# Two attentions keep unscaled probabilities; a block of ones beside the values gives the row sums in the other 64 partitions, VectorE divides once a head

## The reference, cut to what matters

```python
# latent attention: 8 heads, 96 wide queries and keys, 64 wide values, 512 x 512 scores a head
sc = jnp.einsum('bqhd,bkhd->bhqk', qi, k) * scale
p = jax.nn.softmax(sc, axis=-1).astype(v.dtype)
return jnp.einsum('bhqk,bkhd->bqhd', p, v)

# neighbourhood attention: 8 heads of 64, a window of 8 rows x 16 columns of keys, with a bias
sc = jnp.einsum('bnqhd,banchd->bhnqac', qb, kb) * scale + bias[None]
sc = jnp.where(col_valid[None, None, :, :, None, :], sc, -jnp.inf)
p = jax.nn.softmax(sc, axis=(-2, -1)).astype(v.dtype)
o = jnp.einsum('bhnqac,banchd->bnqhd', p, vb)
```

## Time and profile before

| | us |
|---|---|
| median of 3 runs | 3701.93 |
| lowest, highest run | 3698.83, 3705.82 |
| the profiled execution | 3697.52 |
| its span, first to last instruction | 3695.7 |
| PE busy | 3154.2 (85%) |
| DVE busy | 1556.0 (42%) |
| ACT busy | 1083.0 (29%) |
| POOL busy | 962.2 (26%) |
| DVE, the multiplications of L658 in these four attentions, x128 | 141.2, mean 1103 ns |

### The profile page before, as it was taken

How to read it: one execution, slowest core, us unless ns; L and a number is a source line. 1 busy time by engine, 2 the same in 40 slices (tenths; PEclk the granted TensorE clock), 3 DMA queues, 4 the chain that set the end, 5 groups by cost and what they waited for, 6 DMA issues and landing times.

```text
span 3695.7 us, 32882 instructions
## 1 busy us (share of the span) xinstructions
PE 3154.2 (85%) x12970; PEld 2158.7 (58%) x12970; DVE 1556.0 (42%) x2571; ACT 1083.0 (29%) x1563; POOL 962.2 (26%) x329
## 2 busy tenths in 40 slices
PE   5888997867777755999999879996999999879996
PEld 4666654652222224676665568885767674568885
DVE  8895645441011025444455542213353545642213
ACT  3422304210000012444526222212452625322221
POOL 2362200201000012433212223432443211124441
PEclk9889899878999986999999989998999999989998
DMA  5114320237999981212121112221212121112220
GB/s 228 69 57 160 148 80 23 80 137 315 422 422 422 422 345 39 70 57 80 46 80 45 47 69 93 101 92 59 89 52 80 46 80 46 36 67 103 92 103 34
DMA packets 70077, 465.26 MB, mean 126 GB/s; under 512 B 8656, under 2 KB 8944, under 8 KB 17712
## 3 DMA queue, kind: packets, MB, share of 16 engines
q1 hardware_dynamic: 59184, 436.29, 30.7%
q0 software_dynamic: 5056, 16.55, 1.3%
q10 hardware_dynamic: 5696, 10.49, 0.8%
HBM read 450.70 MB, written 12.60 MB: 125 GB/s over the span
## 4 chain that ended last, share of the span: by engine, by line
PE 64%; DVE 16%; DMA 12%; ACT 3%; issue 2%; POOL 1%; SPq 0%; ACTq 0%; DVEq 0%; POOLq 0%
PE ps L414 13%; PE ps L416 12%; PE ps L415 12%; DMA mring<-w 10%; PE ps L403 4%; PE ps L632 3%; PE ps L615 2%; PE ps L616 2%; PE ps L617 2%; PE ps L746 2%; PE ps L2017 1%; PE ps L643 1%; DMA wring<-wfirst 1%; POOL w_lo L471 1%; DVE rnn L1592 1%
## 5 line engine op out<-in xcount | busy, mean ns | idle before, releaser
L471 POOL TENSOR_TENSOR w_lo<-wring,w_hi 128x2048 fp32r<-128x2048 f32 x176 | 816.3, 4641 | 1906.8 <-ACT w_hi L463 1906.7
L414 PE MATMUL ps<-x_hi,w_hi 128*128 128x512 f32 (+1 forms) x1512 | 615.2, 407 | 50.7 <-POOL w_lo L471 28.8
L416 PE MATMUL ps<-x_hi,w_lo 128*128 128x512 f32 (+1 forms) x1512 | 602.9, 399 | 0.0
L463 ACT ACTIVATE w_hi<-wring 128x2048 fp32r<-128x2048 f32 x176 | 335.6, 1910 | 556.0 <-PE ps L414 392.1
L415 PE MATMUL ps<-xf_lo,w_hi 128*128 128x512 f32 x1112 | 441.8, 397 | 0.0
L414 PEld LDWEIGHTS ps<-x_hi,w_hi 128*128 128x128 f32 (+1 forms) x1512 | 293.0, 194 | 130.0 <-issue 38.1
L416 PEld LDWEIGHTS ps<-x_hi,w_lo 128*128 128x128 f32 (+1 forms) x1512 | 292.7, 194 | 63.6
L2017 PE MATMUL ps<-mring,xT__89 128*64 128x512 f32 x512 | 244.8, 609 | 66.2 <-DMA mring<-w 61.2
L2018 PE MATMUL ps<-mring,xT__89 128*64 128x512 f32 x512 | 245.0, 609 | 0.0
L415 PEld LDWEIGHTS ps<-xf_lo,w_hi 128*128 128x128 f32 x1112 | 214.9, 193 | 43.3
L1835 DVE TENSOR_TENSOR hid<-ps,sil 64x512 f32<-64x512 f32 x32 | 21.8, 682 | 441.6 <-ACT sil L1488 441.6
(11 more groups left out here) (412 smaller groups left out, 5333.8 us busy)
## 6 DMA issues: line engine op xcount, KB each, us to landing
mring<-w SPq DMA_DIRECT2D x192, 1024.0 KB, 28.5
wring<-wlayers SPq DMA_DIRECT2D x148, 1024.0 KB, 4.8
wring<-wfirst SPq DMA_DIRECT2D x60, 1024.0 KB, 4.9
wmodS<-wmod SPq DMA_DIRECT2D x4, 2048.0 KB, 18.5
y_rows<-ysb ACTq DMA_DIRECT2D x64, 128.0 KB, 6.4
rp<-rpb POOLq DMA_DIRECT2D x16, 192.0 KB, 2.6
hT<-xT SPq DMA_DIRECT2D x1, 2048.0 KB, 18.3
xS<-xT SPq DMA_DIRECT2D x1, 2048.0 KB, 7.7
```

What stands on the lines that cost most here:

```text
L414: said(pe.matmul(bank, wh[:, 0:m], hi[:, k, :], start=(k == 0), stop=False))
L416: ins = pe.matmul(bank, wl[:, 0:m], hi[:, k, :], start=False, stop=(k == nk - 1))
L463: act.activation(w_hi[:, q % HI_SLOTS, :], wring[:, g % SLOTS, :], ACT.Copy).then_inc(hi_rdy, 1)
L471: pool.tensor_tensor(w_lo[:, slot % SLOTS, :], wring[:, slot % SLOTS, :], w_hi[:, q % HI_SLOTS, :].bitcast(F32), ALU.subtract).then_inc(lo ...
```

## The change: what it does

In units marked "summed" (neighbourhood and latent attention):

- ScalarE's exponential no longer accumulates a row sum, and VectorE's norm of each unit (L657, L658) is not run. The transposes wait for the exponential alone.
- total writes into pair B, and beside each product with the values it runs a product with a 128x64 block of ones into the other 64 partitions of the same bank. These then hold, 64 times over, the row sum of each query.
- VectorE runs divide(h) once a head: the reciprocal of these 64x512 sums from PSUM into o2, then its product with the 64x512 result in PSUM. It stands behind the maximum of unit 4h+6, and for the last head behind the loop.
- ScalarE doesn't copy the head's result; it only waits for the total before it overwrites PT2.
- heads_split stands ahead of the wait for the last gate tile.

In the neighbourhood attention the product with ones takes up to 512 queries at once: three of them a head (512, 512 and 256 columns), beside the ten of 128 columns with values.

```diff
@@ units_pe
-                    pe.wait_ge(p_norm, k + 1)
+                    if "summed" in u:
+                        pe.wait_ge(exp_done, k + 1)
+                    else:
+                        pe.wait_ge(p_norm, k + 1)
@@ units_dve
+            def divide(h):
+
+                r = 64 * (h % 2)
+                b = B.take(dve)
+                after(dve, dve.reciprocal(o2[r:r + 64, h // 2, :], b[64 - r:P - r, :]), dve_step, "dstep")
+                dve.tensor_tensor(o2[r:r + 64, h // 2, :], b[r:r + 64, :], o2[r:r + 64, h // 2, :], ALU.mult).then_inc(B.free, 1)
+                dve.wait_ge(B.free, B.took)
...
-                if i >= 1:
+                if i >= 1 and "summed" not in u:
                     norm(i - 1)
-            norm(U - 1)
+                if i >= 6 and i % 4 == 2 and "summed" in u:
+                    divide(u["h"] - 1)
+            if "summed" in u:
+                divide(u["h"])
+            else:
+                norm(U - 1)
@@ units_act
+                    if "summed" in u:
+                        act.activation(Pb[:, k % 3, 0:n], src, ACT.Exp, bias=negmax[:, k % 4:k % 4 + 1], scale=sc).then_inc(exp_done, 1)
...
-                    sums(units[i - 3])
+                    if sums is not None:
+                        sums(units[i - 3])
+                    else:
+                        act.wait_ge(B.full, pv_before + units[i - 3]["h"] + 1)
@@ na_units
-                    b = A.claim(pe)
-                    for n, (lo, hi) in enumerate(NA_KEYS):
-                        for j in range(lo, hi):
-                            ins = pe.matmul(b[r:r + 64, n * P:(n + 1) * P], v2[:, j, h * 64:(h + 1) * 64],
-                                            PT2[:, j - lo, n * P:(n + 1) * P], start=(j == lo), stop=(j == hi - 1))
-                    ins.then_inc(A.full, 1)
+                    b = B.claim(pe)
+                    x, width = PT2, max(hi - lo for lo, hi in NA_KEYS)
+                    for j in range(width):
+                        wide = [n for n, (lo, hi) in enumerate(NA_KEYS) if hi - lo > j]
+                        q = slice(wide[0] * P, (wide[-1] + 1) * P)
+                        pe.matmul(b[64 - r:P - r, q], ones[:, 0:64], x[:, j, q], start=(j == 0), stop=(j == width - 1))
+                        for n in wide:
+                            lo, hi = NA_KEYS[n]
+                            ins = pe.matmul(b[r:r + 64, n * P:(n + 1) * P], v2[:, lo + j, h * 64:(h + 1) * 64], x[:, j, n * P:(n + 1) * P],
+                                            start=(j == 0 and n == 0), stop=(j == width - 1 and n == wide[-1]))
+                    ins.then_inc(B.full, 1)
@@ mla_units
-                    b = A.claim(pe)
+                    b = B.claim(pe)
                     for j in range(NQB):
-                        ins = pe.matmul(b[r:r + 64, :], vM[:, j, h * 64:(h + 1) * 64], PT2[:, j, :], start=(j == 0), stop=(j == NQB - 1))
-                    ins.then_inc(A.full, 1)
+                        pe.matmul(b[r:r + 64, :], vM[:, j, h * 64:(h + 1) * 64], PT2[:, j, :], start=(j == 0), stop=(j == NQB - 1))
+                        ins = pe.matmul(b[64 - r:P - r, :], ones[:, 0:64], PT2[:, j, :], start=(j == 0), stop=(j == NQB - 1))
+                    ins.then_inc(B.full, 1)
@@ layer_act
-            def mla_out(u):
-                r = 64 * (u["h"] % 2)
-                act.activation(o2[r:r + 64, u["h"] // 2, :], A.take(act)[r:r + 64, :], ACT.Copy).then_inc(A.free, 1)
-            units_act(act, mla_units(), mla_out, P2, PT2, ml_gates)
+            units_act(act, mla_units(), None, P2, PT2, ml_gates, pv_before=B2 + l * B_LAYER + B_MLA)
@@ layer_dve
             units_dve(dve, mla_units(), P2)
-            a += HEADS + DC - EARLY
+            a += DC - EARLY
+            heads_split()
             dve.wait_ge(A.free, a)
-            heads_split()
```

More of the change, by code:

```diff
@@ L675, in units_dve, with units_act @@
                     dve.tensor_scalar(m, m, u["scale"], None, ALU.mult).then_inc(mx_rdy, 1)
-                if i >= 1:
+                if i >= 1 and "summed" not in u:
                     norm(i - 1)
-            norm(U - 1)
+                if i >= 6 and i % 4 == 2 and "summed" in u:
[4 more added lines that the diff above has]
+                norm(U - 1)
             cnt["dv2"] += U
-        def units_act(act, units, sums, Pb=Pb, PT=PT, between=None):
+        def units_act(act, units, sums, Pb=Pb, PT=PT, between=None, pv_before=None):
             U = len(units)
@@ L692, in units_act @@
                     src, sc = (Lb[:, k % 2, 0:n], 1.0) if "bias" in u else (ps[:, 4 + k % 2, 0:n], u["scale"])
-                    act.activation(Pb[:, k % 3, 0:n], src, ACT.Exp, bias=negmax[:, k % 4:k % 4 + 1], scale=sc,
-                                   accum_out=rsum[:, k % 4:k % 4 + 1]).then_inc(exp_done, 1)
+                    if "summed" in u:
+                        act.activation(Pb[:, k % 3, 0:n], src, ACT.Exp, bias=negmax[:, k % 4:k % 4 + 1], scale=sc).then_inc(exp_done, 1)
+                    else:
+                        act.activation(Pb[:, k % 3, 0:n], src, ACT.Exp, bias=negmax[:, k % 4:k % 4 + 1], scale=sc,
+                                       accum_out=rsum[:, k % 4:k % 4 + 1]).then_inc(exp_done, 1)
                 if between is not None:
@@ L714, in na_units @@
                 for n, (lo, hi) in enumerate(NA_KEYS):
-                    units.append({"nk": hi - lo, "qb": n, "h": h, "scale": NA_SCALE,
+                    units.append({"nk": hi - lo, "qb": n, "h": h, "scale": NA_SCALE, "summed": True,
                                   "q": qk2[r:r + 64, h // 2, n * P:(n + 1) * P], "k": qk2[r:r + 64, 4 + h // 2, lo * P:hi * P],
@@ L1197, in build @@
         A2 = RC + 2 * RC + KVC + 4 + 1 + 1 + RC + 2 * DC + HEADS + HEADS + 2 * NQB + HEADS + 2 * NQB
-        A_LAYER = 4 + 8 + HEADS + DC + 4 + 8 + 4 + DC + MQC + KVC + 1 + HEADS + HEADS // 2 + NQB + HEADS + DC + FFC
+        A_LAYER = 4 + 8 + DC + 4 + 8 + 4 + DC + MQC + KVC + 1 + HEADS + HEADS // 2 + NQB + DC + FFC
+        B2 = 2 + DC + 2 + DC + DC + 2 + 1 + 1 + DC + 2 + 1 + 2
+        B_MLA = HEADS + DC + 8 + 2 * 4 + DC + 2 * 2 + 1 + HEADS
+        B_LAYER = B_MLA + HEADS + DC + DC + 3 + FFC + DC + 3
         cnt["rp"] = 0
```

9 lines of the change are left out of this document (5 added, 4 removed).

## The result

The kernel after takes 3733.26 us (median of 4 runs, 3728.88 to 3733.88), the kernel before took 3701.05 us beside it. The ratio is 1.0086 (95% interval 1.0074 to 1.0098): 27 to 36 us slower. The profiled execution has a span of 3731.8 us, against 3695.7.

What follows compares the result with a forecast made beforehand. PE, busy 85% of the span, was taken as the bound. Neighbourhood +6.25 and latent +11.4 us a layer, +35.3 in two layers, took 3697.5 to 3732.8 us, the median to 3737; range 3700 to 3785.

Steps and rivals of the forecast that it cites:

- stretched multiplications gone: Neighbourhood attention: the norm's multiplications (L658), held until GpSimd's L471 is through, leave PE's path; 5.6 us less a layer.
- wait in 7 heads: Neighbourhood attention: the divide delays the next unit's exponential, so PE waits 0.7 us a head; 4.8 us a layer.
- ones: Products with ones in the totals: 0.3 us a neighbourhood head, 0.1 a latent one; 2.4 and 0.8 us a layer.
- unit 26: Latent attention: the score waiting behind the divide comes 5.96 instead of 3.38 us after T; cost 2.0 us.
- unit 30: Latent attention: the last total comes 7.25 instead of 4.90 us after the scores' start; cost 2.35 us.
- The slope from 4 to 10 elements: Reciprocal's length: 6.0 ns an element, 3.2 us for 512; the 1 to 4 slope gave 4.4; 3.3 taken.
- The rival of the fast reciprocal: Every divide: at one element a step it takes 1.55 us, no head waits; 3698 us, 3691 with free ones; 13%.
- The rival of eight steps an element: Every divide: the reciprocal takes 4.4 us, the high bound at 8.3 ns an element; 14%.
- The clock: Behind each attention a 5.5 us pause halves PE's clock; 1.1 us neighbourhood, 1.3 latent including its last total.
- The rival of the slack: Slack hides the waits in the heads and the clock holds; only stalls, ends and last divides remain; 3712 us; 8%.
- The rival in which the columns of values and ones run in turn: Totals: products with ones and values don't run beside each other; 84 us more, 3821 us; 5%.
- The contention of GpSimd with the divide: Divides held by GpSimd: some three hits a layer of up to 4.5 us on top, inside the range.

Runs made afterwards that it cites:

- no_ones: The kernel after with the products with ones left out in both attentions, the reciprocal reading the rows of values instead, output not divided by the sums: 3734.16 us.
- pieces: The kernel after with each head's divide cut into four pieces of 128 columns behind maxima of following units, the last head's left whole: 3703.53 us.
- warm: The kernel after with idle 128x512 products of constants on PE at the attention ends, 8 in each latent end, 6 of them behind every last total: 3720.48 us.
- copy_recip: The kernel after with a plain copy of the same rows in place of the reciprocal, output not scaled rightly: 3696.25 us.
- twice_recip: The kernel after with the same reciprocal issued twice in a row, result unchanged: 3899.59 us.
- spread: The kernel after with ScalarE's row sums, one 128x4 inversion a head, and four PE products spreading the inverses instead of products with ones: 3700.96 us.

## Why the prediction held, step by step

3737 was predicted, 3733.26 measured. From the first attention on the profiles differ by +33.8 us, the sum was +35.3. The parts fit less well: with what follows it, the neighbourhood attention of layer 0 costs 3.1 us, predicted 6.25, and the latent one 14.1 us, predicted 11.4. The signs came as named: a reciprocal of 3.355 us, no neighbourhood head over 13.4 us, 5.4 us between the last total and the first o_hi matmul. The mechanism was right, and that the total came out this near is in part luck.

| step, us a layer | predicted | measured, layer 0 |
|---|---|---|
| reciprocal 64x512 | 3.3 each | 3.355 each |
| N: stretched multiplications gone | -5.6 | -5.6 |
| N: wait in 7 heads | +4.8 | +4.2 |
| N: last divide | +3.55 | +3.5 |
| N: ones | +2.4 | 0 (no_ones) |
| N: clock behind it | +1.1 | +1.0 |
| L: first units, and 5 gated heads | -0.6 + 2.0 | +2.0 in sum |
| L: unit 26 | +2.0 | +2.0, and 1.5 of clock |
| L: unit 30 | +2.35 | +3.0 |
| L: last divide | +3.55 | +3.5 |
| L: ones | +0.8 | 0 (no_ones) |
| L: clock, last total and behind | +1.3 | +2.1 |

The measured numbers are differences of the rows above to the earlier trace rows. In N the 7 heads are 7 x (13.32 - 12.72), and the stage's +2.1 us is 4.2 + 3.5 - 5.6. In layer 1 the stages are +0.7 and +14.8: before lost some 1.5 us to a fall of the clock inside its N1 and none in the last total of its L1. In L a gated head, one with gate pieces beside it, takes 15.01 to 15.03 instead of 14.50 us.

- **The reciprocal.** The slope from 4 to 10 elements was the right one of the two. From 128 to 512 elements it is (3351 - 956) / 384 = 6.24 ns an element (pieces). The rival of the fast reciprocal said 3698 or 3691; with a copy in its place it is 3696. The rival of eight steps an element, at 4.4 us, is excluded.
- **The waits.** The arithmetic of slack, divide plus bias, maximum and exponential against the time until PE wants the score, held for the steady heads within 0.15 us. The unit 26 wait was put at 5.96 us from the start of the scores behind the total to the score that waits; it is 2055.17 - 2049.28 = 5.89.
- **Unit 30** was put 0.65 us too low, and for a reason that could have been read from the code: ScalarE's order puts the copy of unit 29's transposed block behind the exponential of unit 31, and the last transposes need the bank that it frees. Before, the norm ran on DVE beside that copy (0.50 us); without the norm PE waits for the copy itself, at 2069.01.
- **The ones** were taken for 3.2 us a layer too much. Their price was a guess between bounds, and the lower bound was true.
- **The clock** was right in kind and too small in the latent attention: 1.3 us were put down for the last total and the pause behind it; the pauses behind units 26 and 30 make it fall earlier, and it came to 3.7 us in layer 0, 1.5 behind unit 26, 0.1 in the transposes of unit 31, 1.2 in the last total and 0.9 behind the attention. With the 1.6 us that the last total had lost in the kernel before that is 5.3 us, and warm gives back 5.0 (4.1 + 0.9). The prediction put these 1.6 us down to the reason of the long pause in rows 7; but the last total of layer 1 in the same kernel stands behind the same short pauses and takes 3.65 us, so the pause alone doesn't settle it. This error and that of the ones nearly cancel, so the total came out better than its terms.

The rival of the slack (3712) fell: the chain shows the waits, and copy_recip takes them away. The rival in which the columns of values and ones run in turn fell with no_ones. The contention of GpSimd with the divide, an open cost in the range, doesn't show: eight of the 32 reciprocals have a GpSimd L471 beside them for 1.4 us, four of these have other GpSimd work for some 2 us more, and all 32 take 3.35 or 3.36 us. The row of L670 that the prediction took as its sign (0.42 us at 1510.92) could not tell, as GpSimd does nothing at that time.

## What to carry to other kernels

A long instruction on an engine that is half idle costs by its length ahead of the next thing that another engine waits for, not by its share of the engine. Compare that length with the slack, the time until the other engine wants the result. Above the slack each us costs a us, and where TensorE's pause brings its clock down it costs more: 1.55 us for each us of the second reciprocal here (166 of 107). If the work can't be made shorter, cut it into pieces behind several short steps, and look what stands behind the last piece: work for the next stage that is ready (here three of four tiles) belongs ahead of it.

## What the runs showed of the hardware

- Pauses of PE of 0.5 us in every head leave the granted clock at 1.00 (after, 1583 to 1590). Behind pauses of 3.0 and 4.5 us it was 0.50 for a stretch of 2 to 5.5 us (after), and with a pause of 3.9 us in every neighbourhood head it fell in every one of them (twice_recip). Behind pauses of 1.1, 0.3 and 0.7 us it fell in layer 0 of before (last total 5.25 us) and not in layer 1 (3.65 us), so the length of a pause alone did not tell. Idle products in the long pauses keep it at 1.00, and the latent attentions are 4 us shorter (warm).
- A product with a 128x64 block of ones into the other 64 partitions of a bank costs no time beside those with 64 columns of values, even where it is 512 columns wide and they are 128: 13.3 and 15.0 us a head with it and without (after, no_ones). Eight records of 128 columns behind most of the values' products did cost 0.5 us a neighbourhood head (spread).
- A reciprocal from PSUM takes 956 ns for 64x128 (pieces) and 3355 ns for 64x512 (after), also with GpSimd at work beside it; a copy of the same 64x512 takes 689 ns (copy_recip).
